# Sixty-four HBM-to-HBM copies moved from GpSimd's DMA queue to ScalarE's, spread evenly over its stages

## The reference, cut to what matters

```python
keep = lambda a, w: a[:, a.shape[1] - min(w, a.shape[1]):]
kw_all = jnp.concatenate([s_wk, kwin], axis=1)                      # c_win, 512 rows of 128
kd_all = [jnp.concatenate([d_bufs[2 * g], kd[g]], axis=1) ...]      # d0, d1, d2: 128, 512, 1024 rows of 4 x 128
d_new += [keep(kd_all[g], w), keep(vd_all[g], w)]
```

## Time and profile before

| | us |
|---|---|
| median of 3 runs | 808.8 |
| lowest and highest run | 807.18 and 810.38 |
| span of the profiled execution | 814.1 |
| PE busy in it | 747.8 (92%) |
| DVE busy | 426.0 (52%) |
| ACT busy | 241.2 (30%) |
| POOL busy | 165.2 (20%) |

### The profile page before, as it was taken

The page is one execution under the profiler, slowest core; times in us unless marked ns, Lnnn a source line. Parts: engine busy times, 40 slices in busy tenths (PEclk is TensorE's granted clock), DMA queues, the critical chain, the costliest instruction groups (busy, mean ns, idle before and its releaser), DMA issues.

```text
span 814.1 us, 12675 instructions
## 1 busy us (share of the span) xinstructions
PE 747.8 (92%) x4874; PEld 399.8 (49%) x4874; DVE 426.0 (52%) x958; ACT 241.2 (30%) x601; POOL 165.2 (20%) x202
## 2 busy tenths in 40 slices
PE   6989999988899898999999997999898899999896
PEld 4455545444454333444554654555463455654543
DVE  2213598999967989946253243323654425421214
ACT  6234333233112301123144323333320233242322
POOL 0423311112330232440101022511141001001000
PEclk9989999999999999999999999999998999999999
DMA  8656768889785878598686394867779967846901
GB/s 291 227 188 233 249 223 319 322 317 387 257 299 196 316 227 301 188 325 330 235 311 207 123 394 169 305 250 277 267 275 400 363 244 292 320 156 254 365 12 54
DMA packets 67828, 213.08 MB, mean 262 GB/s; under 512 B 5056, under 2 KB 28784, under 8 KB 61880
## 3 DMA queue, kind: packets, MB, share of 16 engines
q0 software_dynamic: 20320, 142.55, 47.7%
q1 hardware_dynamic: 47288, 69.62, 24.2%
q10 hardware_dynamic: 160, 0.11, 0.0%
HBM read 206.22 MB, written 64.68 MB: 333 GB/s over the span
## 4 chain that ended last, share of the span: by engine, by line
PE 61%; DVE 21%; DMA 7%; issue 6%; ACT 4%; DVEq 0%; ACTq 0%; SPq 0%
PE psum L917 30%; PE psum L847 6%; PE psum L983 6%; PE psum L928 5%; DMA ring<-in_w_in_odd 4%; DVE SA L2344 3%; PE psum L898 3%; DVE ring L2341 2%; DVE KC L2176 2%; PE psum L1072 2%; DVE small L2174 2%; PE psum L1038 2%; DMA ring<-in_cache_a_v,index_a 2%; PE psum L1168 1%; PE psum L1247 1%
## 5 line engine op out<-in xcount | busy, mean ns | idle before, releaser
L917 PE MATMUL psum<-ring,XB 128*128 128x512 f32 (+3 forms) x760 | 328.6, 586 | 3.0 <-DMA ring<-in_w_in_odd 2.0
L917 PEld LDWEIGHTS psum<-ring,XB 128*128 128x128 f32 x760 | 143.7, 194 | 160.1 <-issue 153.8
L983 PE MATMUL psum<-Z,ring 128*128 128x512 f32 x256 | 117.8, 606 | 4.1 <-ACT Z L1659 2.9
L1902 DVE TENSOR_TENSOR RT<-Z,const 128x128 f32<-128x128 f32 (+6 forms) x43 | 11.5, 267 | 137.1 <-ACT Z L1559 113.0
L983 PEld LDWEIGHTS psum<-Z,ring 128*128 128x128 f32 x256 | 47.0, 192 | 64.5 <-issue 64.3
L1559 ACT ACTIVATE Z<-psum,stat 128x512 f32<-128x512 f32 (+3 forms) x38 | 24.1, 635 | 170.9 <-PE psum L917 157.7
L928 PE MATMUL psum<-ring,XB 128*8 128x128 f32 (+3 forms) x1664 | 50.2, 269 | 5.4 <-issue 3.8
L928 PEld LDWEIGHTS psum<-ring,XB 128*8 128x8 f32 x1664 | 41.7, 90 | 23.7 <-issue 22.6
L1723 ACT ACTIVATE SM<-SM,stat 128x128 f32<-128x128 f32 (+4 forms) x56 | 26.9, 480 | 71.0 <-DVE stat L2091 69.9
L1469 ACT COPY NW<-psum 128x512 f32<-128x512 f32 (+1 forms) x56 | 32.7, 584 | 48.1 <-PE psum L847 47.1
L2174 DVE MAX8 small<-KC 8x8 f32<-8x1025 f32 x32 | 38.9, 1217 | 1.7
(11 more groups left out here) (346 smaller groups left out, 891.3 us busy)
## 6 DMA issues: line engine op xcount, KB each, us to landing
ring<-in_w_in_odd SPq DMA_DIRECT2D x9, 2048.0 KB, 15.7
ring<-in_w_in_even SPq DMA_DIRECT2D x6, 2048.0 KB, 12.9
ring<-in_cmp_w SPq DMA_DIRECT2D x4, 2048.0 KB, 12.2
ring<-in_w_in_odd SPq DMA_DIRECT2D x8, 1024.0 KB, 22.2
out_s_d_k<-in_state_d_k POOLq DMA_DIRECT2D x8, 1022.0 KB
out_s_d_v<-in_state_d_v POOLq DMA_DIRECT2D x8, 1022.0 KB
Z<-in_cmp_w POOLq DMA_DIRECT2D x5, 1024.0 KB, 7.8
ring<-in_state_d_v POOLq DMA_DIRECT2D x5, 1024.0 KB, 7.8
```

The source lines that it names most:

```text
L917: last = mm(out[:, 0:n], xT[:, k, t * 128:(t + 1) * 128], w[:, k * n:(k + 1) * n], start=k == 0, stop=k == KT - 1)
L983: last = mm(out[:, h * 512:(h + 1) * 512], w[:, (r % 16) * CH + h * 128:(r % 16) * CH + h * 128 + 128], rowsT[:, at:at + 512], start=r == ...
```

## The change

The table `MOVED_AFTER` and POOL's share in the copies go. ACT counts its 351 events, and after each it issues as many copies as keep it in step: the copy with the number k (from 1) comes after the first event whose number times 64 is at least k times 351, so one after every fifth or sixth event, and the last behind ACT's last event. The copies themselves, their order, the semaphore that counts them and SP's wait for it stay.

```diff
-        MOVED_AFTER = dict(ak=1, ck=1, cv=1, dk=1, wk=1, wv=2, ak0_0=0, ak0_1=0, rows1_2=4, av7_1=3, bv_1=3, bv_3=4,
-                           ck1_1=2, dk0_0=2, dk0_1=2, wk0_1=2, dk2_0=4, dk1_0=2, dk1_1=2, dv0_0=2, dv0_1=2)
...
         @block.scalar
...
-            for event in ORDER:
-                if event[0] in stages:
-                    stages[event[0]](*event[1:])
+            own_events = [event for event in ORDER if event[0] in stages]
+            moves = list(MOVES)
+            for at, event in enumerate(own_events):
+                stages[event[0]](*event[1:])
+                while len(MOVES) - len(moves) < (at + 1) * len(MOVES) // len(own_events):
+                    dst, src = moves.pop(0)
+                    eng.dma_start(dst, src).then_inc(sem("moved"), 16)
...
         @block.gpsimd
         def _(pool):
             pool.wait_ge(sem("index"), 5)
-            moves = list(MOVES)
             for name, queue, parts in items:
                 if queue == "pool":
                     stream(pool, name, parts)
-                    for _ in range(MOVED_AFTER.get(name, MOVED_AFTER.get(name[:2], 0))):
-                        if moves:
-                            dst, src = moves.pop(0)
-                            pool.dma_start(dst, src).then_inc(sem("moved"), 16)
-            for dst, src in moves:
-                pool.dma_start(dst, src).then_inc(sem("moved"), 16)
```

## The result

The changed kernel takes 820.5 us (median of 4 runs, 819.19 to 823.71) against 809.6 us for the kernel before on the same chip (4 runs, 807.18 to 810.58). The ratio is 1.0145, interval 1.0108 to 1.0182: slower by 1.45%, or 10.9 us between the medians. The forecast was 5.6 us. The direction is right, 820.5 lies just inside the range, and the change is nearly twice what was forecast.

The account below looks back on a forecast made before the run. The prediction took PE as the bound (61% of the chain). Its six parts, 1.5 + 0.5 + 4.0 + 1.5 - 3.9 + 2.0 = +5.6 us, added to 808.8 gave 814.4 us, with an 8-in-10 range of 804.5 to 821 us.

Parts of the forecast that it names:

- Part 3: Values of A, 264 to 345 us: added copies delay tiles that PE waits for, +4.0 us, from 0 to 8.
- Part 4: Clock: after the idle times added at A's values, PE runs partly at 1.2 GHz, +1.5 us, from 0 to 3.9.
- Part 6: End: the 61st copy makes stores land late before the last output projection, +2.0 us, from 0 to 5.2.
- Part 1: Issuing 64 copies on ACT at 0.40 us each, mostly hidden in its idle time: +1.5 us, from 0 to 6.4.
- Part 5: Pile-up at 604 us: a weight load lands sooner, saving PE's idle time and slow clock, -3.9 us.
- Part 2: Six copies now come before 88 us; a key tile of A may be late, +0.5 us, from 0 to 2.
- The rival of an ACT stalled by its queue: ACT's issues block behind 2.10 MB copies, 3 us at five places on PE's path: +20.6, 829.4 us; chance 0.08.
- No change: Same bytes, engines free a third of the time, DVE covers A's values: within 0.5%, 809.4 us; chance 0.26.
- Faster: Gathers no longer stand behind copies in POOL's queue, copies take only what others leave: -5.7, 803.1 us; chance 0.17.

Follow-up runs that it names:

- 16: Changed kernel with only its 25th copy whole, issued from ACT, the other 63 tiny: ratio 1.0049 to the kernel before.
- the second profile of before: The kernel before, unchanged, run once more for its profile: 808.41 us, span 806.6.
- 6: Changed kernel with its last four copies issued later (782, 798, 802 and 810 us): 815.6 us, ratio 1.0087 to the kernel before.
- 7: Changed kernel with no copies next to the values of A and the end's copies moved too: 816.4 us, ratio 1.0108 to the kernel before.
- 3: Kernel before with all copies still on POOL, but as near as possible at the changed kernel's times: 813.1 us, ratio 1.0053 to the kernel before.
- 4: Changed kernel without any of the 64 copies and without SP's wait for them: 805.7 us, ratio 0.9952 to the kernel before.
- 15: Kernel before with copies on POOL at the changed kernel's times, only the 25th whole, the others tiny: ratio 0.9961 to the kernel before.
- 2: Changed kernel with all copies on ACT, but at the times that POOL had: 844.4 us, ratio 1.0438 to the kernel before.
- 11: Changed kernel with copies at hand-chosen places where ACT idles and fetches seemed to have slack: 814.6 us, ratio 0.9984 to the kernel before.

## Why the prediction was right or wrong, by its steps

The sign was right and for the reason given: tiles of A's values that landed at the last moment are late beside the copies. The signs that the prediction named for being right all came: 64 short issues on ACT, a sum of waits for the values of A of 9.4 us, the load near 605 in 17.2 us, the full clock near 637, and ACT near 778 released by a store.

What failed is the size of parts 3 and 4, 5.5 us together against 8.8 measured: the delay of one tile by the 25th copy (3.7 taken, 5.0 measured) and above all the slow clock behind it (1.5 taken for the whole stretch, 3.0 measured behind that wait). Part 6 was too small by 1.3 us, part 1 too large by 1.5, and part 5 gave 2.0 us more than forecast. These misses nearly cancel: parts 3 to 6 as measured make 6.2 us beside the 3.6 forecast for them, and with part 1 at 0 all parts but the second come out only 1.1 us above their forecast of 5.1. The rest of the miss is nearly all at the start, where the account has +4.1 us against part 2's 0.5, and its cause is open.

- **Part 1 (+1.5).** Measured 0: tiny copies cost what none cost (0.9958 and 0.9952). Each issue took 0.52 us, not the 0.40 that I took from the earlier trace rows, and it still hides. The rival of an ACT stalled by its queue falls with it.
- **Part 2 (+0.5).** The account has +4.1 us here, but it doesn't measure the copies: the group that starts at 94.59 starts at 94.42 without copies and at 92.23 with tiny ones. PE waits 2.30 us for `c_cmp_k`'s tile against 1.35, but where all copies or all but one are tiny it waits from 0.31 to 1.70, so no share of it can be given to the copies. Where the rest comes from stays open.
- **Part 3 (+4.0).** The distance is 4.55 us at 260.28 and 7.07 at 271.72. Of these 2.5 us the waits for tiles are 1.0 (1.72 us in place of 0.76), the most that the 23rd copy has, where I took 1.5. The other 1.6 are slow matmuls (1.74 us at 268.15 and 1.97 behind it), which stand in 16 as well, where that copy is tiny. The 25th copy: I took a latency of 8.79 us from the earlier trace rows, the engines' 5.2 us for the copy and a slack of 0.8, cut to 3.7. The tile took 13.98 us, which is 8.79 + 5.2: all of the copy's engine time came on top. PE waited 5.02 us. DVE's give-back was 4.1 us (15.20 to 11.06) where I took 2.4, since PE's slow matmuls behind that wait, 1.6 us, vanish too. The 27th and 28th: +1.8 (11.06 to 12.89), where I took 1.2.
- **Part 4 (+1.5).** **The clock is the term most mis-sized.** Behind one wait L1323 took 1.94 us in place of 1.07 and L980's group 5.78 in place of 3.63, together 3.0 us, twice what I gave for all of the stretch. I saw 1.96 us at a wait of 2.01 and should have asked what a wait of 4 to 5 us brings.
- **Part 5 (-3.9).** -5.9: right, and larger, because the second profile of before has an idle time of 4.10 us there, not 2.01. The load's "some 15 us" came out as 17.2.
- **Part 6 (+2.0).** +3.3. Right in place (6 takes it away), wrong in how: I let the stores land late, but their issue was late as well, 14.7 us for 16 stores in place of 8.8. In the earlier trace rows a store whose issue took 20.1 us stood already; I read it as a sign for ACT and not for SP.
- **Left out.** No part had the b values near 400 us. In the change they cost 1.16 us of idle time; in 7 they cost 5, and 7.2 with the slow matmuls behind them.

**The rivals.** "No change" fell by its own point: the tiles had less slack than the copy takes. "Faster" named as its condition that a tile beside a copy is delayed by less than about 1 us; it was 5.0. Its argument that a fetch no longer stands behind a copy in POOL's queue is true (3: fetches behind a copy took 12.01 and 10.42 us) but worth little against the kernel before, whose copies cost it 0.5% in all (4), and is outweighed.

**The queue itself.** My sum priced only the times of the copies and gave their queue nothing. For the 25th copy, the one behind the largest step, 15 against 16 shows that the queue decides: the same copy beside the same tiles costs 0.9% from ACT's and nothing from POOL's. The packets show how: in POOL's queue its packets started behind those of the fetches issued before it, and from ACT's they ran while those fetches weren't through. 2, with all copies at the old times, fits it. For the whole change the queue isn't shown to be most of the loss: 3, from POOL's queue at about the same times, loses 11.1 us up to the end of A's values, more than the change, because there the copies stood right ahead of fetches that had no slack. So a queue decides which fetches a copy delays, and the times decide whether these have slack. The Trainium skill (DMA: Bandwidth & Descriptors, section "Issuing engines are not separate DMA queues") has DMAs of all issuing engines interleave on the same 16 engines, so that another issuer saves only its issue time. The first half agrees with what is seen here (56 packets of fetches beside the copy's 32). Taken as the prediction took it, as a rule for the time, the second half would have 15 and 16, and 2 and the kernel before, take the same time; they differ by 0.9% and 4.4%, and the measurement decides.

**Open.** Why bunched copies cost 35 us from ACT: 21 us of them are the longer waits at the two transfers named in 2, and 13 go away with short pieces, but why the queue makes those waits so long wasn't taken apart. Nor is it shown why every profile of a changed program starts later than the second one of before, or why 11 doesn't reach the time without copies.

## What to carry to other kernels

A bulk copy is paid for by the transfers next to it, so price it by their slack, fetch by fetch, and not by the free share of the DMA engines over the whole kernel. In the queue of the urgent fetches it held up the one issued behind it, in another queue also those issued up to 1.5 us before it. So issue it in their queue, right behind the last one that mustn't be late, and only where the next fetch of that queue has the copy's time to spare; where none has, as in 3, that queue is no better. When a wait on PE's path is added, add the matmuls behind it at the lower clock too, here 3.0 us behind one wait of 5.0; and take a second profile of the kernel before, where the first 100 us of one were 10 us off.

## What the runs showed of the hardware

- One 2.10 MB copy from ACT's queue, 1.5 us behind a 1 MB fetch in POOL's, brought the fetch to 12.94 us and in the change to 13.98; with the copy in POOL's own queue, 2.2 us behind it, the fetch landed after 8.3, and the fetch behind the copy after 12.97.
- In POOL's queue no packet of that copy started until 280.42 us, 6.8 us after its issue, when the fetches ahead of it were all but through. From ACT's queue its packets started 4.3 us after the issue, beside those of fetches issued before it.
- Rows of a DMA that follow one another in memory were joined: 16 and 128 rows gave the same 2464 packets in the copies' queue. In an order that doesn't follow memory the 128 pieces stayed apart (9376 packets).
- The issue of a small store on SP took up to 3.3 us while a large copy from another queue was under way; two of them together took 0.83 us without one.
- Issue of one copy on ACT took 0.52 us where they came singly, whatever the size (0.26 to 2.10 MB), and up to 1.49 us in the bunches of 2.
